# Expert dispatch by a row scatter in expert order, four landing buffers for down weights, and attention in head pairs on row and column tiles

## The reference, cut to what matters

```python
# first block, mixture of experts (32 experts, top 4)
logits = xt @ w_router + b_router
top_v, top_e = lax.top_k(logits, 4);  top_w = softmax(top_v)
g = minimum(xb @ w_gate[e] + b_gate[e], 7.0)
u = clip(xb @ w_up[e] + b_up[e], -7.0, 7.0)
y = ((u + 1) * (g * sigmoid(1.702 * g))) @ w_down[e] + b_down[e]
x = layer_norm(ALPHA * x + g2 * sum_k(top_w[k] * y[k]))
# second block, attention of 8 query heads over 2 key heads
s = q @ k.T * 64 ** -0.5          # 512 queries, 512 + 256 keys
att = softmax(s) @ v
mix = concat(mlstm, att) @ w_out
```

## Time and profile before

| | |
|---|---|
| median of 3 runs | 4301.36 us (4299.62 to 4303.39) |
| the profiled execution | 4298.8 us, span 4297.0 us |
| mean granted clock of PE | 0.889 |
| busy over the span | PE 83%, DVE 45%, POOL 19%, ACT 14% |
| DMA | 1129 MB, mean 263 GB/s |

### The profile page before, as it was taken

The page is one execution under the profiler, slowest core; times in us unless marked ns, Lnnn a source line. Parts: engine busy times, 40 slices in busy tenths (PEclk is TensorE's granted clock), DMA queues, the critical chain, the costliest instruction groups (busy, mean ns, idle before and its releaser), DMA issues. The chain is left out here.

```text
span 4297.0 us, 37357 instructions
## 1 busy us (share of the span) xinstructions
PE 3550.9 (83%) x11892; PEld 1637.7 (38%) x11893; DVE 1945.9 (45%) x4152; ACT 612.9 (14%) x1471; POOL 809.6 (19%) x877
## 2 busy tenths in 40 slices
PE   7988998297999879998829946998987888888876
PEld 3355443232333323333215534774433333333332
DVE  5834222422222222222250255336667667667776
ACT  1011120000000000000001111111222222222222
POOL 2000000200010000110000040001444444444443
PEclk9999999598999989999959966559999999999998
DMA  9723123279988993787751000014999999999998
GB/s 331 282 86 126 49 76 116 76 296 423 366 344 342 364 414 145 294 337 317 306 189 59 0 6 0 1 49 156 414 426 427 410 426 427 417 411 427 413 427 341
DMA packets 179444, 1129.37 MB, mean 263 GB/s; under 512 B 24043, under 2 KB 25483, under 8 KB 59636
## 3 DMA queue, kind: packets, MB, share of 16 engines
q1 hardware_dynamic: 94340, 553.30, 32.9%
q0 software_dynamic: 84992, 574.68, 32.3%
HBM read 1107.21 MB, written 25.55 MB: 264 GB/s over the span
## 5 line engine op out<-in xcount | busy, mean ns | idle before, releaser
L1165 PE MATMUL ps<-e_wt,e_xT 128*64 128x512 f32 x3200 | 743.6, 622 | 112.3 <-DMA e_wt<-in_w_exp 111.6
L2368 DVE SCALAR_TENSOR_TENSOR mod<-q_uv,mix 128x1024 f32<-128x1024 f32 x512 | 627.8, 1226 | 372.3 <-DMA q_uv<-in_peer_uv,q_picks 368.2
L2069 POOL DMA_INDIRECT q_uv<-in_peer_uv,q_picks x512 | 575.9, 1125 | 1111.0 <-PE ps L2165 701.8
L2165 PE MATMUL ps<-q_uv,q_dg 128*128 128x512 f32 x1024 | 512.4, 657 | 134.2 <-ACT q_dg L2242 134.1
L2165 PE MATMUL ps<-q_uv,tri 128*128 128x512 f32 x1024 | 467.8, 611 | 75.8 <-ACT tri L2242 75.7
L1165 PEld LDWEIGHTS ps<-e_wt,e_xT 128*64 128x64 f32 x3200 | 242.7, 144 | 603.4 <-issue 447.7
L1165 PE MATMUL ps<-e_wt,e_aT 128*64 128x512 f32 x1600 | 357.3, 599 | 21.8 <-ACT e_aT L1218 21.8
L2165 PEld LDWEIGHTS ps<-q_uv,q_dg 128*128 128x128 f32 x1024 | 210.5, 211 | 427.3 <-issue 427.3
L2165 PEld LDWEIGHTS ps<-q_uv,tri 128*128 128x128 f32 x1024 | 196.0, 195 | 344.2 <-issue 344.2
L446 PE MATMUL ps<-hT,ring 128*128 128x512 f32 x640 | 285.0, 602 | 1.5 <-DVE qkv L773 1.5
L1124 POOL DMA_INDIRECT scratch_y<-e_yb,e_row x50 | 50.1, 1002 | 974.9 <-DVE e_yb L1280 974.9
(11 more groups left out here) (439 smaller groups left out, 3681.6 us busy)
## 6 DMA issues: line engine op xcount, KB each, us to landing
e_wt<-in_w_exp SPq DMA_DIRECT2D x384, 1024.0 KB, 10.9
ring<-in_w_in_units SPq DMA_DIRECT2D x15, 2048.0 KB, 10.0
mod<-in_w_mod_units SPq DMA_DIRECT2D x48, 512.0 KB, 4.7
mod<-in_w_ada_units SPq DMA_DIRECT2D x32, 512.0 KB, 7.6
p_ring<-in_w_in SPq DMA_DIRECT2D x5, 2048.0 KB, 8.0
c_y<-scratch_y SPq DMA_DIRECT2D x4, 2048.0 KB, 14.6
q_wq<-in_peer_wq_units SPq DMA_DIRECT2D x8, 1024.0 KB, 8.5
q_uv<-in_peer_uv,q_picks POOLq DMA_INDIRECT x512, 12.4
```

Source lines behind the costliest of these rows:

```text
L1165: ins = nc.tensor.matmul(ps[64 * h:64 * h + 64, at, :], lhs[:, k % 4, 64 * (k // 4):64 * (k // 4) + 64], wt[:, u, a, h * W:(h + 1) * W], s ...
L2069: pool.indirect_dma_start(out=uv[:, n % NR, :, :].rearrange("p a d -> p (a d)"), out_offset=None, in_=A["peer_uv"], in_offset=bass.Indirec ...
L2165: last = nc.tensor.matmul(acc(t)[:, c, :], dg(n), uv[:, n % NR, 1, c * W:(c + 1) * W], start=fresh, stop=closing)
L2368: dve.scalar_tensor_tensor(junk[:, n % 2, :], uv[:, n % NR, 0, :], 1.0, mix[:, tile_of(k), :], ALU.mult, ALU.mult, accum_out=ap[:, k % 2, ...
```

## The change

1. **first_mix**: the ring of weights lies in the buffer that later holds the expert weights (`wt`, now allocated in `build`). SP issues, after each of eight of the twelve weight tiles, a copy of 2.13 MB of zeros from DRAM to DRAM into a new array `xs` of 52 x 64 rows of 4 KB.
2. **first_merge**: all work goes token tile by token tile. Positions come from a shorter chain on DVE. h2 is no longer written to DRAM as a whole and there are no slot records: POOL scatters the h2 rows themselves, 16 indirect DMAs of 128 rows x 4 KB, into `xs` in expert order. SP loads the 12 units of expert 0 once the last w_out product is done.
3. **experts**: ACT's queue loads a block (2 DMAs of 64 rows x 2 KB) and stores its result in the same place of `xs`. POOL's gathers and scatters and DVE's scaling go. The down units of the next expert land in four extra buffers `land`, and POOL copies them (128x2048 each, 4 per expert) into `wt` when the last block is done with them.
4. **combine**: POOL gathers the results by position (16 indirect DMAs of 128 x 4 KB), ACT scales them by the routing weights (4 passes of 128x1024 per token tile), and each tile's square root follows its scaling on ACT; DVE normalises tile by tile.
5. **second_heads**: attention in 16 pairs of heads (one of each key head) on three PSUM banks, two buffers. Scores use the two row halves of PE; exponentials are scaled by the reciprocal of their sum on ACT ahead of the transposes; the product has the 64 value columns stationary and the 128 queries moving, the two heads on the two column halves, so that its output is feature-major.
6. **route_peer**: the attention half of `mix` needs no transposes: 4 groups in place of 8. The rows of w_out_2 are permuted on the host.

```diff
# first_merge
@@ SP
-                sp.dma_start(dram["h2"]..., h2[:, :, :]).then_inc(s_h2out, 16)
-                sp.wait_ge(s_h2out, 16)
+                sp.wait_ge(s_full, 8 + 2 * NT)
+                for u in range(NUNIT):
+                    sp.dma_start(wt[:, u]..., A["w_exp"][0, u]).then_inc(s_w[u], 16)
@@ POOL
-                        pool.indirect_dma_start(
-                            out=dram["i_slots"], out_offset=...(ap=pos[:, t, k:k + 1], axis=0),
-                            in_=meta[:, t, k, :], in_offset=None).then_inc(s_slots, 16)
+                        pool.indirect_dma_start(out=dram["xs"], out_offset=...(ap=pos[:, t, k:k + 1], axis=0),
+                                                in_=h2[:, t, :], in_offset=None).then_inc(s_rows, 16)
@@ PE
+                mixed(0); mixed(1); logits(0); mixed(2); logits(1); mixed(3); logits(2)
+                rank(0); rank(1); logits(3); rank(2); rank(3)
@@ DVE
+                tile(0); tile(1); choose(0); tile(2); choose(1); tile(3); choose(2); choose(3)
# experts
@@ SP
                     for u in range(4):
                         unit(u)
-                    ...
-                    for u in range(4, NUNIT):
+                    biases(e)
+                    for u in range(4, 8):
                         unit(u)
+                    for u in range(4):
+                        sp.wait_ge(s_cp[u], e)
+                        sp.dma_start(land[:, u]..., A["w_exp"]...[:, 8 + u, :]).then_inc(s_w[8 + u], 16)
@@ POOL
+                with pool.Fori(1, NE) as e:
+                    done = pool.value_load(blocks[0:1, bass.ds(e + FIRST, 1)], min_val=0, max_val=NBLK)
+                    for u in range(4):
+                        pool.wait_ge(s_w[8 + u], e * 16 + 16)
+                        pool.wait_ge(s_mm[8 + u], done * 2 + 2)
+                        ...
+                        nc.gpsimd.tensor_copy(wt[:, 8 + u], land[:, u]).then_inc(s_cp[u], 1)
@@ PE
-                    pe.wait_ge(s_w[u], e * 16 + 16)
+                    if u < 8:
+                        pe.wait_ge(s_w[u], e * 16 + 16)
+                    else:
+                        pe.wait_ge(s_cp[u - 8], e + 1)
@@ ACT, block i
                             keep(xT[:, 1 - b], XT, s_xt, i + 1, s_xT)
+                            load(i + 2)
                             sigmoid(i)
+                            act.wait_ge(s_y, i + 1)
+                            store(i - 1)
# combine
+                for t in range(NT):
+                    act.wait_ge(s_y[t], 16 * TOPK)
+                    for k in range(TOPK):
+                        last = act.activation(y[:, t, k, :], y[:, t, k, :], ACT.Copy, scale=w4[:, t, k:k + 1])
+                    last.then_inc(s_sc, 1)
+                    act.wait_ge(s_var, t + 1)
+                    act.activation(sd[:, t:t + 1], sd[:, t:t + 1], ACT.Sqrt).then_inc(s_sd, 1)
# second_heads, PE
+                    if n >= 2:
+                        pe.wait_ge(s_aT, n - 1)
+                    for g, c0, k0, nk in ((0, 0, 0, 512), (1, 1024, 256, 512), (0, 512, 512, 256), (1, 768, 0, 256)):
+                        rows = slice(g * DH, (g + 1) * DH)
+                        if (g, nk) == (1, 256):
+                            pe.wait_ge(s_as, 2 * n + 1)
+                        last = nc.tensor.matmul(both(n)[:, c0:c0 + nk], qT[rows, r, t * P:(t + 1) * P], kT[rows, k0:k0 + nk], ...)
...
+                for n in range(PAIRS2):
+                    turn(n)                 # 12 transposes, after s_ap of pair n
+                    if n >= 1:
+                        attend(n - 1)       # 12 products, 64 x 128, after s_aT
+                    if n + 2 < PAIRS2:
+                        scores(n + 2)
# second_heads, ACT
+                exponentials(0)
+                for n in range(PAIRS2):
+                    ...
+                    if n + 1 < PAIRS2:
+                        exponentials(n + 1)  # 2 x 768, after s_am of pair n + 1
+                    act.wait_ge(s_rd, n + 1)
+                    act.wait_ge(s_ae, n + 1)
+                    for g in range(AKV):
+                        last = act.activation(pr[:, n % 2, g, :], pr[:, n % 2, g, :], ACT.Copy, scale=rd[:, n % 2, g:g + 1])
+                    last.then_inc(s_ap, 1)
# second_heads, DVE
+                for n in range(PAIRS2):
+                    ...
+                    dve.tensor_copy(pT[:, n % 2]..., both(n)).then_inc(s_aT, 1)   # 128 x 1536
+                    if n + 1 < PAIRS2:
+                        denominators(n + 1)
+                    if n + 2 < PAIRS2:
+                        maximum(n + 2)       # 128 x 1536
```

More of the change, by code:

```diff
@@ L937, in _ @@
-                last.then_inc(s_rank, 1)
+                    last.then_inc(s_rank, 1)
+                mixed(0)
+                mixed(1)
+                logits(0)
+                mixed(2)
+                logits(1)
+                mixed(3)
+                logits(2)
+                rank(0)
+                rank(1)
+                logits(3)
+                rank(2)
+                rank(3)
             @block.scalar
             def _(act):
-                for n in range(1, 3):
-                    act.wait_ge(s_var, n)
-                    act.activation(sd, sd, ACT.Sqrt).then_inc(s_sd, 1)
@@ new lines, in keep @@
+                def keep(t):
+                    for b in range(2):
+                        act.wait_ge(s_turn, 2 * t + b + 1)
+                        act.copy(h2T[:, 4 * b:4 * b + 4, t * P:(t + 1) * P],
+                                 ps[:, 2 * t + b, :].rearrange("p (k q) -> p k q", k=4)).then_inc(s_h2T, 1)
+                for t in range(NT):
+                    root(2 * t)
+                    root(2 * t + 1)
+                    if t >= 1:
+                        keep(t - 1)
+                keep(NT - 1)
@@ L1001, in _ @@
-                for t in range(NT):
-                    link(dve.max(v8[:, t, :], lg[:, t, :]))
-                    link(dve.max_index(i8[:, t, :], v8[:, t, :], lg[:, t, :]))
+                dve.wait_ge(s_const, 16 * 5)
+                dve.memset(run[:, :, :], 0.0)
+                link(dve.tensor_scalar(thr[:, :], iot[:, 0:T // BLK], float(BLK), None, ALU.mult))
+                tile(0)
+                tile(1)
+                choose(0)
+                tile(2)
+                choose(1)
@@ new lines, in _ @@
+                link(dve.tensor_reduce(run[:, 0, PAD:], full[:, :, :], AX_X, ALU.add))
+                link(dve.tensor_copy(cnt[:, 1, :], run[:, 0, PAD:]))
+                for a in range(5):
+                    src, dst = run[:, a % 2], run[:, 1 - a % 2]
+                    link(dve.tensor_tensor(dst[:, PAD:], src[:, PAD:], src[:, PAD - (1 << a):PAD + NE - (1 << a)], ALU.add))
+                total = run[:, 1, PAD:]
+                link(dve.tensor_tensor(cnt[:, 0, :], total, cnt[:, 1, :], ALU.subtract))
@@ L1152, in _ @@
+                for u in range(4):
+                    pool.wait_ge(s_cp[u], NE)
             @block.tensor
@@ L1712, in turn, with attend @@
                     last.then_inc(s_at, 1)
+                def attend(n):
+                    t, r = n // REP, n % REP
+                    pe.wait_ge(s_aT, n + 1)
+                    if r == 0 and t >= 2:
+                        pe.wait_ge(s_av, t - 1)
+                    for j in range(NA):
+                        for g in range(AKV):
+                            last = nc.tensor.matmul(ps[g * DH:(g + 1) * DH, 6 + t % 2, r * P:(r + 1) * P],
+                                                    zr[:, j, 656 + g * DH:656 + (g + 1) * DH], pT[:, n % 2, g * NA + j, :],
+                                                    start=(j == 0), stop=(j == NA - 1))
+                            if j == NA - 1:
+                                last.then_inc(s_ao, 1)
@@ L1755, in _, with exponentials @@
                 act.copy(kT[:, T:], ps[:, 5, 0:TC]).then_inc(s_qT, 1)
-                for n in range(NT * AHEADS):
-                    if n == 4:
-                        act.wait_ge(s_var, 1)
-                        act.activation(rs[:, :], rs[:, :], ACT.Sqrt).then_inc(s_sd, 1)
-                    base = 2 * (n % 3)
-                    t, hh = n // AHEADS, n % AHEADS
+                def exponentials(n):
                     act.wait_ge(s_am, n + 1)
```

557 lines of the change are left out of this document (240 added, 317 removed).

## The result

The changed kernel takes 4270.8 us (median of 4 runs, 4268.7 to 4275.1) against 4302.4 for the kernel before, measured beside it: a ratio of 0.9925, 95% interval 0.9908 to 0.9943. It is 32 us faster, where 86 were forecast.

| stretch | before, us | after, us | change | forecast |
|---|---|---|---|---|
| first_mix, to the start of first_merge | 647.3 | 648.8 | +1.5 | 0 |
| first_merge to the first gate product | 216.9 | 187.9 | −29.0 | −53.7 |
| first gate product to combine | 1295.1 | 1260.5 | −34.6 | −63.5 |
| combine | 50.7 | 63.8 | +13.1 | +11 |
| second_project | 260.9 | 263.3 | +2.4 | 0 |

A forecast was written before the change was run, and what follows sets the result against it. Bounds: DVE and PE taking turns in dispatch, PE pace and weight waits in experts, PE at half clock in attention. Terms −53.7 − 62 − 1.5 + 11 + 20 = −86 gave 4215 us, range 4143 to 4273.

The forecast's parts named there:

- combine's price: Combine: scaling and sums in series at 12.3 us per tile, 61 us in all, +11 us, bounds +3 and +16.
- the safe copy: Experts: GpSimd's 128x2048 copy taken as 3.8 us, below the point of 4 to 4.5 us.
- (c): Attention: row or column halves do not overlap, for instance because scores wait on one bank; 4265 us, chance 0.1.
- (d): Dispatch: scatter of 4 KB rows runs at half of 427 GB/s and ends 20 us later; 4235 us, chance 0.12.
- (e): Experts: landing buffers do not help since DMA is at its rate; only expert 0's 12 us stay; 4265, chance 0.09.
- dispatch: First_merge to first gate product: only the last token tile's work stays exposed, gate at 810.5; −53.7 us.
- experts: Experts stage: landing buffers remove the weight wait at ten run starts, expert 0 lands ahead; −62 us, stage end −1.5.
- route_peer: Route_peer: 16 transposes less (3.4 us) lie under the load of the peer keys; 0 us.
- attention: Second_heads: steps of a pair in series at half clock, 15.0 us per pair, 16 pairs 240 us; +20 us.
- the rule: Experts: hand-stepped weight arrivals through 50 blocks; stage 1265 us before, 1211 after for a copy below 4 us.
- rival (a): Attention: PE runs at full clock, 11.0 us per pair, −40 us instead of +20; 4155 us, chance 0.15.
- Rival (b): Experts: the GpSimd copy takes 7 us and the kernel is slower than before; 4343 us, chance 0.04.

The follow-up runs named there:

- Experiment 1: Changed kernel with ScalarE copying the transposes of tile t-1 before the roots of tile t in first_merge: 4245.1 us.
- experiment 8: Changed kernel without token-row loads from the fourth block on: 4237.0 us; also with one load and store DMA of 128 rows, 4628.2, and four load DMAs, 4268.5.
- 5: Changed kernel with pos and w4 allocated behind the weight buffer, so weight and gather buffers start at multiples of 512 bytes: 4240.2 us.
- 6: Changed kernel with SyncE issuing the four bias rows after the four up units instead of ahead of them: 4259.0 us.
- 7: Changed kernel without landing buffers, down units going straight to their place and GpSimd copying nothing: 4285.4 us.
- experiments 3 to 5: Third: changed kernel giving pos and w4 back after combine, 4250.6 us. Fourth: kernel before plus an unused 128 bytes per partition, 4325.9 us, timed again 4319.4.

## Why the prediction was wrong in size and right in sign

The sign, the series of steps in the attention, combine's price and the safe copy held. The time lies in the range, close to its upper edge of 4273, but that is luck: the range was stretched so far for rivals (c), (d) and (e), and none of them came about as told, while what did cost time, ScalarE's order and a buffer's address, was not among the rivals. The change is 32 us where 86 were forecast. Three terms were too good (dispatch by 25, experts by 29, route_peer by 22), and attention, off by 24 the other way, hid part of it. Dispatch and experts lie outside their own bounds (35 to 62, and 45 to 75).

**Dispatch, 25 us short.** The step "three tiles of four hide under w_out. Only the last tile is exposed" took each engine's work as free to move. Its condition was not checked on ScalarE's list, which puts the copy of tile t−1 behind two roots of tile t. Experiment 1 shows it: with the order turned, 22 us come back, and the rest of the step is right to 4 us.

**Experts, 29 us short.** The first step that failed is the hand-worked run start, "landed by +1; gate units land at 3.6 to 10.9, wanted at 7.3 to 12.5: no loss". In the trace of the changed kernel, with the end of the down at 1177.3, the four landing units are in at 1174.0 to 1183.5 and the gate units at 1186.4 to 1193.8, that is 9 to 16.5: 5.5 us later than worked out. The block costs 4.35 more than 22.27 and not nothing. Half of the delay is a late start: the rule has the last gate unit at 10.9, and the first up unit landed 11 units of 2.45 us ahead of it, at 1161.2 in this trace, but it landed at 1164.1. The other half is the pace, 2.70 us a unit from there to 1193.8. Of the 4.35 us the runs name 1.6 for the loads, priced at "a little for gathers" (experiment 8), 0.3 for units that are 0.05 us slower off the grid (5) and 0.5 for the late request behind the biases (6); the remaining 2 are not shown singly. And "within a longer run ... nothing is gained there" was too kind: 1.33 us are lost in each of eight blocks, 0.4 of them to the grid (5). The rest is laid to the loads on ScalarE's queue, which cost 1.34 there (8), against the gathers on GpSimd's; that is argued, as no run leaves the gathers out of the kernel before. The landing buffers themselves are worth 2.7 us at a run start (7), where the sum had 4.2 (62 − 8, less some 12 for expert 0, over ten). Of those 12, 2.8 came, from the first gate to the first down. Against all this the end of the stage gave 9.4 us in place of 1.5, a piece of luck. By bytes, both kinds of load are equal; the gathers and scatters moved them in packets of 4096 bytes (median 159 ns), the loads and stores in packets of 2048 (94 ns over the stage), and that accounts for only part of it. Why the rest, is open. Rival (e) is out: without landing buffers the stage is 22.6 us longer (7).

**Attention, 24 us better.** The order of steps is as forecast and the rival of overlapping steps is out, but "at half clock" held in most pairs for two of TensorE's three parts only. Scores took 2.42 us instead of 4.1, and 1.7 us in each of 16 pairs are 27 us; in the one pair at half clock throughout they took 4.20. So it is neither the forecast nor rival (a), but between them: 13.5 us where the two said 15.0 and 11.0. The tiles of a pair do run together: 24 records of products in 2.83 us with the clock at 0.50, where the 12 of the kernel before took 2.66; rival (c) is out.

**route_peer, "nothing", 22 us.** The transposes did hide (TensorE still waits for the peer keys). The prediction put the whole stage at nothing, but a change can move a buffer it does not touch: 128 bytes that are not given back cost these 22 us (experiments 3 to 5).

**Combine** was 2 us off. **Copy:** 1.90 us against the 3.8 that was taken from the strided L379, and against the 3.1 us estimated from the Trainium skill (GPSIMD Engine Reference, 3.1): for this plain copy both are too high, and the measurement decides. Rival (b) never came near. Rival (d), the scatter at half rate, is out too: 16 scatters issued from 801.55 to 823.4 were followed by the first load 8 us later, and their 8.39 MB took 22.4 us (805.0 to 827.5), where half the rate needs 39. The zeros in first_mix show as the 1.5 us of the table, and that is within what four profiles of the stage without them differ by (646.6 to 649.6 us).

## What to carry to other kernels

When work is regrouped into tiles, write down for each engine the list of what it issues in order, and ask at every wait which later item of another tile stands behind it: two swapped lines on ScalarE were worth 22 and 78 us here, more than the whole change. Keep large DMA destinations in SBUF at multiples of 256 bytes, and give small arrays back or put them behind the large ones: one 128-byte shift cost 1.7% of the DMA rate in route_peer, which DMA bounds, and 2% of the pace of the weight units. Let the pattern of a DMA begin with its rows and not with a dimension of 2, and check by the 4-byte packets how many engines it got. Price a small transfer beside a saturated queue by leaving it out once, not by its bytes.

## What the runs showed of the hardware that was not expected

- A destination buffer 128 bytes off the 256-byte grid: 413 in place of 420 GB/s, 8 KB packets with a mean of 316.5 in place of 311.9 ns, 22 us over 1411.
- One DMA of 128 rows as a pattern of 2 x 64 x 512 in place of two DMAs of 64 rows: from 4271 to 4628 us, with the same bytes and packets of the same size, but 2 packets of 4 bytes for a DMA in place of 16, and two of the 16 DMA engines at work by that count.
- GpSimd copies 128x2048 float32 in 1.90 us, while the smaller strided copy of 128x1024 took 1.97.
- TensorE's granted clock changed within a pair of heads, 0.50 under transposes and products and 0.94 under scores; with the pair cut from 13.5 to 7.9 us in the mean it was at 0.83 over the whole of the attention, where in the kernel before, with hardly a wait at all (215 of 217 us busy), it stayed at 0.50.

```profile
2669.00:2886.00 217.00, 215.33 (x704) 158.45 (x703) 83.54 (x153) 34.52 (x67) 0.00 (x0) 0.50 0.00 1
```
